# Page loads of the second cache set wait for half of the prompt's attention scores, not for all of them

## The chip, the cores and the metric

The kernel runs on one core of a Trainium2 chip. The metric is the device time of one execution in microseconds; lower is better. Three runs of the kernel before gave 1573.28, 1573.8 and 1576.76 us, so the median is 1573.8 us.

## The reference, cut to what matters

One layer of a hybrid decoder is computed for a prompt of 1040 tokens (16 meta tokens and 1024 of its own) and for 8 samples of 4 new tokens each. The part that matters here is the latent attention with 8 heads. For the prompt it is causal attention over its own tokens; for the samples it reads a paged cache of 4096 past tokens for each sample:

```python
def mla_sample(q_lat, q_rope, ckv_new, krope_new, cache_ckv, cache_krope, page_table):
    past_ckv = cache_ckv[page_table].reshape(Bd, -1, MLA_KV_LORA)      # 8 x 4096 x 256
    past_kr = cache_krope[page_table].reshape(Bd, -1, MLA_ROPE)        # 8 x 4096 x 32
    s_past = einsum('bthc,bsc->bhts', q_lat, past_ckv) + einsum('bthr,bsr->bhts', q_rope, past_kr)
    ...
    p = softmax(s * MLA_SCALE)
    return einsum('bhts,bsc->bthc', p[..., :P], past_ckv) + ...
```

Ahead of it stand the input projection and the gated linear attention, behind it the output projection, two normalisations and a gated feed-forward block with a short convolution.

## The kernel before, in words

Every engine runs one list of instructions, in order, and waits on semaphores (counters) that the others raise. Two stages matter.

**Prompt attention** (called d in the code). It has `N_ATT` = 66 steps: two for the last 16 tokens, and then, for each of 4 pairs of heads, 16 steps (8 blocks of 128 queries in the order 7, 0, 6, 1, 5, 2, 4, 3, for each of the two heads). In a step TensorE multiplies queries and keys (`scores`, L1268) and raises `score_done`; VectorE adds the mask and takes the maximum (L1389); ScalarE takes the exponentials (L1329) and raises `probs_done`; TensorE turns the probabilities (L1282); ScalarE and VectorE copy them out of PSUM (`ptb`, L1349 and L1402); and after both heads of a pair TensorE turns the reciprocals of the row sums (`rs`, L1291) and multiplies by the values (L1305). ScalarE then copies the reciprocals out of PSUM (`rb`, L1357), and VectorE multiplies them into the result (`catT`, L1435), which frees the bank for the next stage. TensorE issues scores two steps ahead of the step whose probabilities it turns. At the end of the stage there is no next step to run ahead with.

**Decode attention** (called e). The cache is read in `SETS` = 16 sets, z = 0 to 15; a set is 4 gathers of 512 KB (`load_latents`, L1534), one for each of 4 samples, issued by GpSimd (POOL), which also generates the descriptors. The rotary part comes in 4 groups of 4 gathers of 256 KB (`load_rotary`, L1541). A set lands in one of `SLOTS` = 3 slots `ring_c`, of 16 KB in each partition. The slots lie over memory of the stage before: slot 1 (sets 1, 4, ...) lies at `E0`, where `qT`, the prompt's queries, begins. `qT` has 8 heads of 4288 bytes, so slot 1 covers heads 0 to 3, all but the end of head 3. Slot 2 covers the rest of head 3 and most of the others.

For each set TensorE turns the pages (L1622), ScalarE and VectorE copy them out (`pastT`, L1727 and L1719), TensorE computes scores (L1643), turns the probabilities (L1655) and multiplies by the pages (L1669). Two steps on the samples' own new tokens come first. TensorE turns set 0 at once, and set 1 as the next step.

What GpSimd issues, in this order: the 4 gathers of set 0 (during the preparation of attention), `load_rotary(0)`, then a wait for `score_done` >= 33 and `load_rotary(1)`, then set 1, set 2, and so on, each behind `slot_free`. For set 1 that is a wait for all 66 scores, since the scores read `qT`. For set 2 the list has a wait of its own for `ss_done` >= 2, the first two scores of the decode stage. From set 3 on a slot is free when the values of the set in it are done.

Of the kernel before, what the change touches and what calls it, by code (L numbers as in the profile page):

```python
# [102 lines left out]
def build(nc, ins, outs):  # L103
    with ExitStack() as ctx:
# [8 lines left out]
        def sem(name):  # L113
            return ctx.enter_context(nc.semaphore(name))
# [1087 lines left out]
        score_done = sem("score_done")  # L1202
# [14 lines left out]
        N_ATT, N_JOBS = len(att_steps), len(att_jobs)  # L1217
# [290 lines left out]
        def step_of(z):  # L1508
            return z + 2
# [5 lines left out]
        def slot_free(eng, z):  # L1515
            if z == 0:

                eng.wait_ge(prep_done, index[("ckv", NT - 1)] + 1)
                eng.wait_ge(latent_stored, 96)
            if z == 1:  # L1520

                eng.wait_ge(score_done, N_ATT)
            if z >= SLOTS:

                eng.wait_ge(spv_done, step_of(z - SLOTS) + 1)
# [34 lines left out]
        def pool_e(pool):  # L1560
            pool.wait_ge(pages_ready, 2)
            slot_free(pool, 0)
            load_latents(0)
            out_of_psum(pool, prep[-1])
            load_rotary(0)
            pool.wait_ge(score_done, N_ATT // 2)
            load_rotary(1)
            for z in range(1, SETS):
                slot_free(pool, z)
                if z == 2:  # L1570
                    pool.wait_ge(ss_done, 2)
                if z < SLOTS:
                    load_latents(z)
                    continue
                load_latents(z, (0,))
                if 4 <= z < 12:
                    q = 1 + z // 4
                    if z % 4 == 0:
                        pool.wait_ge(rope_packed, R_SETS * (q - 1))
                    load_rotary(q, (z % 4,))  # L1580
                pool.wait_ge(ss_done, step_of(z - 2) + 1)
                load_latents(z, (1,))
                pool.wait_ge(past_turned, N_TURN * (z - 1) + 3)
                load_latents(z, (2,))
                pool.wait_ge(past_turned, N_TURN * (z - 1) + SPLIT_TURN)
                load_latents(z, (3,))
# [1482 lines left out]
```

## Time and profile before

| | |
|---|---|
| median of 3 runs | 1573.8 us |
| profiled execution, its own time | 1568.31 us |
| its span from first to last instruction | 1566.7 us |
| mean granted TensorE clock | 0.979 |
| TensorE busy | 95% of the span |
| prompt attention, from the first maximum to the last score | about 419 to 568 us |
| decode attention | about 577 to 743 us |

The durations below are from the profiled execution. It was 5.5 us (0.35%) shorter than the median of the runs, so a sum is made against 1568.31 and then carried over to 1573.8. In a row of the timeline the first number is the start in us from the start of the span, the second the duration in us; the brackets give how long the engine was idle before it and what ended the wait. "issue" and "remote" stand where the profile names no engine as the releaser.

### The profile page before, as it was taken

How to read it: one execution, taken by the hardware profiler on the slowest of the kernel's cores; microseconds unless marked ns; L12 is line 12 of the kernel's file. 1: busy time of each engine (PE TensorE's matmuls, PEld its weight loads, DVE VectorE, ACT ScalarE, POOL GpSimd, SP SyncE). 2: the span in 40 equal slices, each digit the busy share in tenths (PEclk: the TensorE clock that was granted, in tenths of full speed). 3: DMA queues.
4: the chain of work that ended last, by engine and by line, in shares of the span. 5: the costliest groups of instructions: out<-in, count | busy, mean ns of one | idle time of the engine just before them, and what ended most of it. 6: DMA issues, size and time to landing. Idle time of an engine off the chain costs nothing.

```text
span 1566.7 us, 29052 instructions
## 1 busy us (share of the span) xinstructions
PE 1486.0 (95%) x11025; PEld 1258.8 (80%) x11025; DVE 1002.7 (64%) x1733; ACT 655.6 (42%) x1232; POOL 346.1 (22%) x391
## 2 busy tenths in 40 slices
PE   5999999889899989999999999999999999999994
PEld 5989998656566666666788999999999998678883
DVE  6615302655455555556668888888888885456685
ACT  2255322543355543335222555555554443435330
POOL 2101000200000013441011144444444443110011
PEclk9999999889899999999999999999999999999997
DMA  7221101201100036776124255555555557978462
GB/s 259 82 69 59 55 28 42 72 4 54 42 1 28 1 107 216 238 245 219 68 94 110 82 188 185 173 178 167 184 180 177 168 175 258 359 237 307 151 200 94
DMA packets 121205, 217.63 MB, mean 139 GB/s; under 512 B 10922, under 2 KB 67880, under 8 KB 118264
## 3 DMA queue, kind: packets, MB, share of 16 engines
q1 hardware_dynamic: 97994, 120.89, 23.9%
q0 software_dynamic: 22976, 95.43, 17.4%
q8 instruction: 62, 1.02, 0.3%
q14 instruction: 29, 0.24, 0.0%
q10 hardware_dynamic: 144, 0.07, 0.0%
HBM read 165.66 MB, written 50.69 MB: 138 GB/s over the span
## 4 chain that ended last, share of the span: by engine, by line
PE 61%; DVE 6%; issue 3%; DMA 2%; ACT 1%; POOL 1%; SPq 0%; another core or an unknown queue 0%; ACTq 0%; DVEq 0%; POOLq 0%
PE ps L2280 9%; PE ps L2279 9%; PE ps L2278 9%; PE ps L1268 4%; PE ps L1622 3%; PE ps L2904 3%; PE ps L2906 3%; PE ps L2905 3%; PE ps L1643 3%; PE ps L1305 2%; PE ps L210 2%; PE ps L212 2%; PE ps L211 2%; PE ps L1282 2%; PE ps L1669 2%
## 5 line engine op out<-in xcount | busy, mean ns | idle before, releaser
L2278 PE MATMUL ps<-t_hi,op_hi 128*128 128x266 f32 (+1 forms) x672 | 192.2, 286 | 2.4 <-DVE gap_hi L2502 2.4
L2280 PE MATMUL ps<-t_hi,op_lo 128*128 128x266 f32 (+1 forms) x672 | 192.9, 287 | 0.0
L2279 PE MATMUL ps<-t_lo,op_hi 128*128 128x266 f32 (+1 forms) x672 | 192.7, 287 | 0.0
L210 PE MATMUL ps<-w_hi,hT_hi 128*128 128x256 f32 (+2 forms) x504 | 141.8, 281 | 3.4 <-DVE hT_lo L324 3.4
L2280 PE MATMUL ps<-h1T_hi,op_lo 128*128 128x266 f32 x504 | 144.1, 286 | 0.0
L2278 PE MATMUL ps<-h1T_hi,op_hi 128*128 128x266 f32 x504 | 143.5, 285 | 0.0
L2279 PE MATMUL ps<-h1T_lo,op_hi 128*128 128x266 f32 x504 | 143.4, 285 | 0.0
L212 PE MATMUL ps<-w_hi,hT_lo 128*128 128x256 f32 (+2 forms) x504 | 141.2, 280 | 0.0
L211 PE MATMUL ps<-w_lo,hT_hi 128*128 128x256 f32 (+2 forms) x504 | 141.1, 280 | 0.0
L2731 DVE TENSOR_TENSOR ring_lo<-d_raw,ring_hi 128x1024 fp32r<-128x1024 f32 x77 | 95.3, 1248 | 56.0 <-ACT ring_hi L2727 55.0
L2278 PEld LDWEIGHTS ps<-t_hi,op_hi 128*128 128x128 f32 x672 | 127.4, 190 | 2.6 <-DVE gap_hi L2502 2.6
L2727 ACT ACTIVATE ring_hi<-d_raw 128x1024 fp32r<-128x1024 f32 x77 | 81.7, 1061 | 112.2 <-DMA d_raw<-t_res 57.4
L2279 PEld LDWEIGHTS ps<-t_lo,op_hi 128*128 128x128 f32 x672 | 127.7, 190 | 0.0
L2280 PEld LDWEIGHTS ps<-t_hi,op_lo 128*128 128x128 f32 x672 | 127.4, 190 | 0.0
L2904 PE MATMUL ps<-ring_hi 128*128 128x512 f32 x308 | 121.6, 395 | 2.1 <-DVE ring_lo L2731 1.2
L2905 PE MATMUL ps<-ring_lo,ring_hi 128*128 128x512 f32 x308 | 120.2, 390 | 0.0
L2906 PE MATMUL ps<-ring_hi,ring_lo 128*128 128x512 f32 x308 | 119.9, 389 | 0.0
L2403 DVE TENSOR_TENSOR op_lo<-s_sum,op_hi 128x512 fp32r<-128x512 f32 x84 | 106.2, 1303 | 0.0
L1534 POOL DMA_INDIRECT ring_c<-in_cache_ckv,row_at x64 | 60.3, 942 | 188.7 <-PE ps L1268 69.9
L210 PEld LDWEIGHTS ps<-w_hi,hT_hi 128*128 128x128 f32 x504 | 96.8, 192 | 3.9 <-DVE hT_lo L324 3.8
L212 PEld LDWEIGHTS ps<-w_hi,hT_lo 128*128 128x128 f32 x504 | 97.3, 193 | 0.0
L211 PEld LDWEIGHTS ps<-w_lo,hT_hi 128*128 128x128 f32 x504 | 96.7, 192 | 0.0
(366 smaller groups left out, 3574.9 us busy)
## 6 DMA issues: line engine op xcount, KB each, us to landing
f_raw<-in_w_ffn_in SPq DMA_DIRECT2D x88, 256.0 KB, 3.3
g_res<-gap_lo SPq DMA_DIRECT2D x22, 528.0 KB, 3.6
g_mix<-in_w_down POOLq DMA_DIRECT2D x11, 1024.0 KB, 5.3
t_res<-g_mix POOLq DMA_DIRECT2D x11, 1024.0 KB, 4.2
g_mix<-g_res POOLq DMA_DIRECT2D x11, 1024.0 KB, 5.2
s_res<-g_mix POOLq DMA_DIRECT2D x11, 1024.0 KB, 4.2
d_raw<-in_w_down SPq DMA_DIRECT2D x22, 512.0 KB, 7.0
d_raw<-s_res SPq DMA_DIRECT2D x44, 256.0 KB, 3.6
```

The costliest lines, as they stand in the source:

```text
L210: nc.tensor.matmul(out, ah, bh, start=start, stop=False)
L211: nc.tensor.matmul(out, ah, bl, start=False, stop=False)
L212: return nc.tensor.matmul(out, al, bh, start=False, stop=stop)
L2278: nc.tensor.matmul(o, ah, bh, start=FIRST_IN[q] and k == 0, stop=False, skip_group_check=again)
L2279: nc.tensor.matmul(o, ah, bl, start=False, stop=False, skip_group_check=again)
L2280: last = nc.tensor.matmul(o, al, bh, start=False, stop=k == 3, skip_group_check=again)
L2403: nc.vector.tensor_tensor(op_lo[q][:, :, :], OP_OF[q], op_hi[q][:, :, :].bitcast(F32), sub).then_inc(op_split, 1)
L2727: nc.scalar.activation(ring_hi[m % RING][:, :], d_raw[raw_slot[m]][:, 0:1024], ACT.Copy).then_inc(d_high, 1)
L2731: nc.vector.tensor_tensor(ring_lo[m % RING][:, :], d_raw[raw_slot[m]][:, 0:1024], ring_hi[m % RING][:, :].bitcast(F32), sub).then_inc(d_sp ...
L2904: nc.tensor.matmul(b, ah, bh, start=j == 0 and not again, stop=False, skip_group_check=again)
L2905: nc.tensor.matmul(b, ah, bl, start=False, stop=False, skip_group_check=again)
L2906: last = nc.tensor.matmul(b, al, bh, start=False, stop=j == NJ - 1, skip_group_check=again)
```

## The change

Set 1 no longer waits for all 66 scores but for 2 + 33 = 35 of them. The two tail steps and the 32 steps of the first two head pairs come first, so once 34 scores are done nothing reads heads 0 to 3 of `qT` any more. Set 2, which had relied on set 1's wait standing ahead of it in the same list, gets the wait for all 66 scores itself.

```diff
             if z == 1:
 
+                eng.wait_ge(score_done, 2 + N_ATT // 2)
+            if z == 2:
+
                 eng.wait_ge(score_done, N_ATT)
             if z >= SLOTS:
```

No instruction is added, removed or put at another place in any engine's list. In GpSimd's list set 1 stands directly behind `load_rotary(1)` before and after; only the count that its first gather waits for differs, and the first gather of set 2 waits for two semaphores in place of one.

## Rows read from the trace of the kernel before

**Rows 1.** The page: busy time of the engines, then shares of the last chain
```profile
PE 1486.0 (95%) x11025; PEld 1258.8 (80%) x11025; DVE 1002.7 (64%) x1733; ACT 655.6 (42%) x1232; POOL 346.1 (22%) x391
...
PE 61%; DVE 6%; issue 3%; DMA 2%; ACT 1%; POOL 1%; SPq 0%; another core or an unknown queue 0%; ACTq 0%; DVEq 0%; POOLq 0%
```

**Rows 2.** Busy time by stretch: length, PE PEld DVE ACT POOL, clock, DMA, GB/s
```profile
540.00:555.00 15.00, 14.63 (x128) 10.53 (x125) 8.08 (x25) 8.25 (x26) 0.00 (x0) 1.00 0.01 2
...
640.00:680.00 40.00, 38.35 (x389) 23.96 (x388) 23.08 (x51) 14.97 (x34) 18.92 (x20) 1.00 0.75 241
```

**Rows 3.** Timeline of GpSimd: rotary group 1, set 1, set 2
```profile
493.51 0.95 POOL L1541 DMA_INDIRECT ring_r<-in_cache_krope,rope_at  x1 [79.46 <-PE ps L1268]
...
568.15 0.94 POOL L1534 DMA_INDIRECT ring_c<-in_cache_ckv,row_at  x1 [69.93 <-PE ps L1268]
...
578.72 0.94 POOL L1534 DMA_INDIRECT ring_c<-in_cache_ckv,row_at  x1 [5.88 <-PE ps L1643]
```

**Rows 4.** Busy time by microsecond, after set 1's gathers were issued
```profile
575.00:576.00 1.00, 1.00 (x14) 0.82 (x10) 0.00 (x0) 0.00 (x0) 0.00 (x0) 0.51 0.88 344
...
577.00:578.00 1.00, 0.92 (x40) 0.82 (x40) 0.61 (x3) 0.00 (x0) 0.00 (x0) 0.50 0.02 8
...
582.00:583.00 1.00, 1.00 (x11) 0.99 (x10) 0.53 (x1) 0.69 (x2) 0.69 (x2) 1.00 0.96 324
```

**Rows 5.** Timeline of TensorE, ScalarE and VectorE from prompt to decode attention
```profile
569.72 1.31 PE L1305 MATMUL ps<-ptb,v_h 128*64 128x128 f32 x20
570.96 0.66 PE L1282 MATMUL ps<-consts,probs 128*128 128x128 f32 x4
...
572.48 0.28 ACT L1357 ACTIVATE rb<-ps 128x128 f32<-128x128 f32 x1 [2.17 <-PE ps L1305]
572.86 0.29 DVE L1435 TENSOR_TENSOR catT<-ps,rb 128x128 f32<-128x128 f32 x1 [3.71 <-ACT rb L1357]
...
573.26 0.23 DVE L1417 COPY rs<-rinv 128x128 f32<-128x128 f32 x1
573.54 0.33 PE L1291 MATMUL ps<-consts,rs 128*128 128x128 f32 x1 [1.92 <-issue]
573.95 0.60 ACT L1349 ACTIVATE ptb<-ps 128x512 f32<-128x512 f32 x1 [1.20 <-remote]
574.60 1.62 PE L1305 MATMUL ps<-ptb,v_h 128*64 128x128 f32 x16 [0.74 <-ACT ptb L1349]
576.26 0.28 ACT L1357 ACTIVATE rb<-ps 128x128 f32<-128x128 f32 x1 [1.71 <-PE ps L1305]
...
577.08 0.44 PE L1643 MATMUL ps<-ckvT,qlat 128*32 128x32 f32 x16 [0.86 <-DVE catT L1435]
...
578.35 3.65 PE L1622 MATMUL ps<-consts,ring_c 128*128 128x128 f32 x16
...
589.25 1.97 PE L1622 MATMUL ps<-consts,ring_c 128*128 128x128 f32 x16
```

**Rows 6.** Timeline: the same value products within the attention, without a gather
```profile
534.57 1.31 PE L1305 MATMUL ps<-ptb,v_h 128*64 128x128 f32 x20
...
535.92 0.28 ACT L1357 ACTIVATE rb<-ps 128x128 f32<-128x128 f32 x1 [0.76 <-PE ps L1305]
...
503.66 1.09 PE L1305 MATMUL ps<-ptb,v_h 128*64 128x128 f32 x16
...
504.80 0.28 ACT L1357 ACTIVATE rb<-ps 128x128 f32<-128x128 f32 x1
```

**Rows 7.** Timeline of VectorE: first maxima of head pairs 2 and 3
```profile
499.27 1.23 DVE L1389 CUSTOM_DVE_ANT_0 ps<-ps,wide 128x1024 f32<-128x1024 f32 x1 [2.23 <-PE ps L1268]
...
501.77 1.23 DVE L1389 CUSTOM_DVE_ANT_0 ps<-ps,wide 128x1024 f32<-128x1024 f32 x1 [1.07 <-PE ps L1268]
...
534.12 1.23 DVE L1389 CUSTOM_DVE_ANT_0 ps<-ps,wide 128x1024 f32<-128x1024 f32 x1 [1.03 <-PE ps L1268]
...
537.83 1.23 DVE L1389 CUSTOM_DVE_ANT_0 ps<-ps,wide 128x1024 f32<-128x1024 f32 x1 [1.23 <-PE ps L1268]
```

## The prediction

> **What bounds the kernel now.** I read the page first. TensorE is busy for 95% of the span, and its work is by far the largest part of the chain that ended last [rows 1]. By stretches the same holds on both sides of the change: 14.63 of 15 us busy in the middle of the prompt attention with the DMA engines nearly still, 38.35 of 40 us in the decode attention at 241 GB/s [rows 2]. So a load can only matter where TensorE waits for it, or where it disturbs a hand-over on which TensorE waits.
>
> Next the timeline of GpSimd. Set 1's first gather was issued at 568.15, the end of a wait of 69.93 us for the last score [rows 3]. By the busy time of each microsecond its transfer still ran at 344 GB/s at 575 and was over at 577 (8 GB/s) [rows 4]. TensorE turns set 1 only at 589.25 [rows 5]. The set is ready 12 us before it is read. **As a load, the change saves nothing**: the 12 us of slack become about 80. Set 2 is issued at 578.72, released by the decode stage's own first scores [rows 3], and its new wait for score 66 was met 10 us before that. It costs nothing, even if the decode stage starts some us earlier.
>
> What is left is where the 2 MB of set 1 travel. Before, they travel between 568 and 577, exactly where the prompt attention runs out. There the timeline of the three engines shows two hand-overs that come late [rows 5]. The 20 value products start at 569.72 and last 1.31, so they end at 571.03; ScalarE's copy of the reciprocals, which waits for them, starts at 572.48. Within the attention, with no gather, the same pair is 534.57 + 1.31 = 535.88 and 535.92 [rows 6], so 0.04 us is usual and 1.41 us was lost. Then TensorE turns the last probabilities from 570.96 to 571.62, and ScalarE, free from 572.76, takes them only at 573.95.
>
> **The change, part by part.**
>
> 1. *The end of the prompt attention without a gather.* All by rows 5. The copy of the reciprocals would start at 571.03 + 0.04 = 571.07 and end at 571.35. VectorE's product followed its start by 0.38, and the end of the copy to `rs` (573.49) came 1.01 behind it: 572.08. ScalarE would take the turned probabilities at about 571.66, and end 0.60 later, at 572.26. In the trace the last 16 value products start 0.05 behind the end of that copy (573.95 + 0.60 = 574.55, then 574.60), so here at 572.31; `rs` at 572.08 would be turned by then or cost 0.1 more. That is 2.3 us less. The lower bound of this term is zero, if the late hand-overs have another cause; no row shows this place without a gather.
>
> 2. *The clock in it.* From 575 the granted clock is 0.51, then 0.50, that is 1.2 GHz, and it is back at 1.00 (2.4 GHz) in the row of 582 [rows 4]. Before it fell TensorE had idled 1.92 and 0.74 us [rows 5]. The last 16 value products took 1.66 us from their start to the copy that follows (574.60 to 576.26), against 1.14 (503.66 to 504.80) at the full clock [rows 6]: 0.5 us. The first 16 transposes of the decode stage took 3.65 us, those of set 1 at the full clock 1.97 [rows 5]: 1.7 us, of which I count 1.6, because copies out of PSUM then follow more closely. With term 1 the idle times shrink to about 0.5 and 0.8 us (the second is 576.26 + 0.28 to 577.08, of which nothing changes, and a little more). I take it that the clock holds then, so 2.1 us for this term; zero if it falls all the same.
>
> 3. *The same 2 MB within the attention.* The gather now goes out when 35 scores are done. The 35th is the first of head pair 2, whose maximum VectorE starts at 499.27 [rows 7]; GpSimd has issued the four of `load_rotary(1)` by then (from 493.51 on [rows 3]). So the first gather of set 1 is issued at about 499.4, and as the transfer before ended some 9 us after its first issue (568.15 to 577 [rows 3, 4]), this one ends at about 508. The trace has one gather just ahead of this place already, that of the rotary part, half as large. It too makes a hand-over late: VectorE starts the first maximum of pair 2 at 499.27, 2.50 us before the second at 501.77; in pair 3, without a gather, the distance is 534.12 to 537.83, so 3.71 [rows 7]. It came 1.21 us late, and the next one was on time, so it cost nothing: TensorE had two steps of scores to run ahead with. What is behind a late hand-over here is VectorE's maximum, ScalarE's exponentials and copies, and TensorE's turn of the probabilities two steps on. The price of 2 MB lies between nothing (as for the 1.21 us) and the whole of what they cost where there is no running ahead, 2.3 us. I take 0.4, near the row at the same place, because TensorE idles only 0.37 of 15 us [rows 2], and a hand-over that is 1.4 us or more late may exceed what it can cover.
>
> 4. *Rows that stay.* The instructions, their order, the bytes and the decode stage's own gathers are the same; 15 of 16 sets travel with the same neighbours.
>
> Sum: -2.3 - 2.1 + 0.4 = **-4.0 us**. Against the profiled execution that is 1568.31 to 1564.3; its distance to the median is taken as kept, so 1573.8 - 4.0 = **1569.8 us**, 0.25% less. About 0.2% (3.1 us) is what a measurement of this kernel can tell from no change, for the three runs alone spread over 3.5 us. The forecast is near that edge.
>
> The Trainium skill, "SBUF — State Buffer", section "SBUF: two separate sides", speaks against all of this. It says that engine ports and DMA ports to that memory are disjoint and cannot contend. By that rule a gather delays no compute, the late hand-overs of rows 5 and 7 must have another cause, and terms 1 to 3 are all nothing. The trace does not agree with it taken widely: it shows late starts in both places. But it may be right about the memory, if what is late is the signal.
>
> **The rivals.**
>
> *The clock falls all the same.* For it: about 1.3 us of idle time remain within 3 us. Against it: smaller idle times within the attention leave 1.00 [rows 2]. Then only terms 1 and 3 count, with or without the 0.5: -1.9 to -2.4, so 1571.4 to 1571.9 us.
>
> *Nothing happens.* The set was hidden before and is hidden after, and the late hand-overs belong to the drain of a stage (or to the taking of the profile) and not to the gather; this is also the case by the skill's rule above. For it: two of the three late ones stand at the drain. Against it: the third stands in the steady part, and there, too, a gather is under way. 1573.8 us, give or take 1.
>
> *Slower.* The gather's late hand-overs fall into the attention and are not covered. The place is the four or five steps from 499 to 508, where TensorE is the bound. If each of the four gathers delays one hand-over by up to 2.3 us with nothing to run ahead with, that is 9.2 us; less the gain at the end (4.4) it is +4.8, so 1578.6 us. The point from which it decides is a loss of 4.4 us there for any slowdown, and of 7.5 us for one that can be measured. Against it: the 1.21 us of rows 7 were covered in full.
>
> *In between.* The gain at the end is real, and the loss in the attention eats half of it or all: 1571.5 to 1573.8 us.
>
> **How the numbers follow.** Forecast as summed: 0.38. Clock falls all the same: 0.19. Nothing: 0.22. In between: 0.11. Slower: 0.10. Of the forecast and the clock case 0.40 lie beyond 0.2% on the fast side. Of the other cases a tenth of the whole may come out beyond it on the slow side, and a little more by scatter between measurements; I say faster 0.40, same 0.47, slower 0.13. The range runs from 1568 (term 3 at nothing, and a little of the decode start) to 1576.5 (half of the slower case, and scatter of the median), and leaves out the rest of the slower case and the far ends. The forecast's own range is 1568 to 1571.
>
> **What the new profile would show.** GpSimd issues set 1 from about 499.4 on. In the last steps of the prompt attention the copy `rb` follows the value products by 0.04 us, ScalarE's last `ptb` follows the turn at once, and the decode scores start about 2.8 us earlier, measured from the last score. The clock stays at 1.00 there, and the first 16 transposes take about 2 us. Between 499 and 508 some maximum or copy starts over 1 us late, but the distance from the first maximum of pair 2 to that of pair 3 grows by no more than 1 us. The forecast is wrong if the drain has the same late hand-overs without a gather in it, if the clock falls anyway, or if pair 2 grows by 3 us or more.

## The result, and the profile after

The changed kernel took **1576.88 us** (median of 20 runs, 1572.2 to 1582.97), the kernel before 1573.26 us (20 runs, 1569.24 to 1576.76). The ratio is **1.0031, 95% interval 1.0021 to 1.0042**; the two medians alone give 1.0023, the two means 1.0032. That is 0.2 to 0.3% slower where 0.25% faster was forecast, and 0.4 us outside the stated range. Two later comparisons of the same two kernels gave 0.9998 and 0.9997, and the kernel before against its own copy gave 1.0018 and 0.9997. So the change is a small loss to nothing, not the gain of 4 us. It does move time about inside the kernel, and that can be read in the traces, though each trace is one execution only.

The profiled execution took 1580.67 us. The page gives for it, as [rows 1] for before, the busy time of the engines and the shares of the last chain:

```profile
PE 1493.1 (95%) x11025; PEld 1263.9 (80%) x11025; DVE 1000.7 (63%) x1733; ACT 655.6 (42%) x1232; POOL 346.5 (22%) x391
...
PE 61%; DVE 6%; issue 2%; DMA 2%; ACT 1%; POOL 1%; SPq 0%; another core or an unknown queue 0%; ACTq 0%; DVEq 0%; POOLq 0%
```

Totals tell nothing here: the same work, a span 12.4 us longer, of which 5.4 had gathered before the prompt attention began (its first maximum starts at 425.36, against 419.93). What the change does is read from distances within one trace: from the first maximum at L1389 on VectorE, which is that of the first head pair, to the first decode score; from the last maximum to it; and from it to the end of the last product with the pages.

| one profiled execution | first maximum to decode | last maximum to decode | decode to last product |
|---|---|---|---|
| before | 157.15 | 9.16 | 165.98 |
| changed | 160.14 | 6.44 | 167.34 |

**The end of the attention.** The timeline of TensorE and ScalarE in the changed kernel, where [rows 5] stood before:

```profile
580.87 1.31 PE L1305 MATMUL ps<-ptb,v_h 128*64 128x128 f32 x20
582.11 0.66 PE L1282 MATMUL ps<-consts,probs 128*128 128x128 f32 x4
582.23 0.28 ACT L1357 ACTIVATE rb<-ps 128x128 f32<-128x128 f32 x1 [0.76 <-PE ps L1305]
...
582.81 0.60 ACT L1349 ACTIVATE ptb<-ps 128x512 f32<-128x512 f32 x1 [0.30 <-PE ps L1282]
...
583.29 0.33 PE L1291 MATMUL ps<-consts,rs 128*128 128x128 f32 x1 [0.52 <-DVE rs L1417]
583.55 1.09 PE L1305 MATMUL ps<-ptb,v_h 128*64 128x128 f32 x16
584.69 0.28 ACT L1357 ACTIVATE rb<-ps 128x128 f32<-128x128 f32 x1 [1.28 <-PE ps L1305]
...
585.50 0.33 PE L1646 MATMUL ps<-ckvT,qlat 128*32 128x32 f32 x16 [0.86 <-DVE catT L1435]
...
586.42 1.97 PE L1625 MATMUL ps<-consts,ring_c 128*128 128x128 f32 x16
```

The products end at 582.18 and the copy `rb` starts 0.05 behind them, where it was 1.45 behind. The last 16 products take 1.14 to the copy behind them, where it was 1.66, and the transposes of set 0 take 1.97, where it was 3.65. The clock did not fall. The end of the attention is 9.16 - 6.44 = 2.72 us shorter; 2.8 had been worked out.

**The attention.** GpSimd's timeline has set 1 directly behind the rotary gathers, and set 2 again behind the decode stage's first scores ([rows 3]):

```profile
503.97 0.95 POOL L1537 DMA_INDIRECT ring_c<-in_cache_ckv,row_at  x1 [0.31 <-issue]
...
587.29 0.94 POOL L1537 DMA_INDIRECT ring_c<-in_cache_ckv,row_at  x1 [78.63 <-PE ps L1646]
```

And the timeline of the three engines at that time:

```profile
503.51 1.23 DVE L1389 CUSTOM_DVE_ANT_0 ps<-ps,wide 128x1024 f32<-128x1024 f32 x1 [1.03 <-ACT probs L1329]
...
503.95 1.31 PE L1305 MATMUL ps<-ptb,v_h 128*64 128x128 f32 x20
...
505.20 1.98 PE L1268 MATMUL ps<-kT,qT 96*128 96x512 f32 x4
...
507.02 0.60 PE L1282 MATMUL ps<-consts,probs 128*128 128x128 f32 x4
...
510.37 0.28 ACT L1357 ACTIVATE rb<-ps 128x128 f32<-128x128 f32 x1 [5.15 <-remote]
...
510.75 0.29 DVE L1435 TENSOR_TENSOR catT<-ps,rb 128x128 f32<-128x128 f32 x1 [5.94 <-ACT rb L1357]
510.95 1.22 DVE L1389 CUSTOM_DVE_ANT_0 ps<-ps,wide 128x1024 f32<-128x1024 f32 x1
...
511.79 0.49 PE L1268 MATMUL ps<-kT,qT 96*128 96x128 f32 x2 [4.17 <-ACT probs L1329]
```

Three pieces of TensorE's work end at 505.26, 507.18 and 507.62 by their rows (the ends of matmuls are modelled). What waits for the first, the copy `rb`, starts at 510.37, with ScalarE idle for 5.15 us and VectorE for 5.94. TensorE then idles 4.17 us itself. The running ahead by two steps was used up. In what follows, "a late signal" stands for this: an engine takes up a result of TensorE long after the row of that work ends. In these rows a signal that came late can't be told from a result that was finished late. By the busy time of each microsecond, TensorE had nothing to do at 509 and the clock fell behind it:

```profile
509.00:510.00 1.00, 0.00 (x0) 0.00 (x0) 0.00 (x0) 0.00 (x0) 0.00 (x0) 1.00 1.11 352
...
512.00:513.00 1.00, 1.00 (x7) 1.00 (x7) 0.75 (x6) 0.96 (x2) 0.00 (x0) 0.63 0.36 148
513.00:514.00 1.00, 1.00 (x6) 0.70 (x4) 0.08 (x1) 0.96 (x3) 0.00 (x0) 0.50 0.03 12
```

Ahead of head pair 2, and from the maximum at 516.54 up to the last one, the distances between neighbouring maxima equal those of before to 0.01 us. So the loss lies in this one place: 160.14 - 157.15 + 2.72 = 5.7 us. Of these, 3.8 are there at the maximum at 510.95, and 2.0 more come up to that at 516.54, while the clock was down. The late start of 1.21 us at the rotary gathers ([rows 7]) is missing in this trace, though the same gathers run: the first maximum of pair 2 follows the last of pair 1 by 503.51 - 501.25 = 2.26 us, against 499.27 - 495.80 = 3.47 before. Where a signal is late is not the same in every execution.

**The decode stage's start.** It gives back part of the gain at the end:

```profile
590.72 0.63 PE L1672 MATMUL ps<-zt,spt 32*32 32x256 f32 x8
...
592.96 0.27 ACT L1730 ACTIVATE spt<-ps 32x128 f32<-32x128 f32 x1 [2.09 <-remote]
593.12 0.42 DVE L1850 COPY oacc<-ps 128x256 f32<-128x256 f32 x1 [0.81 <-remote]
...
593.70 0.66 PE L1672 MATMUL ps<-zt,spt 32*32 32x256 f32 x8 [2.35 <-DVE oacc L1850]
594.28 3.54 PE L1646 MATMUL ps<-pastT,qlat 128*32 128x512 f32 x16
```

```profile
595.00:596.00 1.00, 1.00 (x10) 0.20 (x5) 0.42 (x2) 0.00 (x0) 0.00 (x0) 0.50 1.03 410
```

While set 2 travels (410 GB/s), TensorE's results are taken late again: it idles 2.35 us, and the scores of set 0 then take 3.54 us at a granted clock of 0.50, that is 1.2 GHz; the trace of before has them in 1.92 us at 586.40. The decode part is 1.36 us longer than before although its first transposes were 1.7 us quicker.

### The profile page after: what moved, and what is told of

Same layout as the page of the kernel before. It is cut to its first block, busy times and chain, and to the rows that moved or that the text cites. A ratio compares the mean times of both kernels' runs of the same rounds, so it can differ in the third digit from the quotient of the medians.

```text
span 1579.1 us, 29053 instructions
## 1 busy us (share of the span) xinstructions
PE 1493.1 (95%) x11025; PEld 1263.9 (80%) x11025; DVE 1000.7 (63%) x1733; ACT 655.6 (42%) x1232; POOL 346.5 (22%) x391
## 2 busy tenths in 40 slices
DMA packets 121205, 217.63 MB, mean 138 GB/s; under 512 B 10922, under 2 KB 67880, under 8 KB 118264
## 4 chain that ended last, share of the span: by engine, by line
PE 61%; DVE 6%; issue 2%; DMA 2%; ACT 1%; POOL 1%; SPq 0%; another core or an unknown queue 0%; ACTq 0%; DVEq 0%; POOLq 0%
PE ps L2283 9%; PE ps L2282 9%; PE ps L2281 9%; PE ps L1268 4%; PE ps L1625 3%; PE ps L1646 3%; PE ps L2907 3%; PE ps L2908 3%; PE ps L2909 3%; PE ps L210 2%; PE ps L212 2%; PE ps L211 2%; PE ps L1305 2%; PE ps L1672 2%; PE ps L1282 2%
```

## The experiments

They stand in four groups; each group was timed against the kernel before, on one chip. The kernel before had two levels: 1563.57 us (group 1) and 1563.53 (group 3), 1573.00 (group 2) and 1573.94 (group 4), each group on another chip. In all traces of groups 1 and 3 no signal of TensorE around set 1 is late, in groups 2 and 4 there are late ones. As each chip was met once, chip and moment can't be told apart; "on such chips" below means in such a group. This split turned out to be the main finding, so the groups are told in order. "Distance" is that from the first maximum to the first decode score.

### Group 1: place, amount and issuer

**apart50**: set 1 behind 50 scores.

```diff
             if z == 1:
-                eng.wait_ge(score_done, 2 + N_ATT // 2)
+                eng.wait_ge(score_done, 50)
```

> The changed kernel with the 4 gathers of set 1 waiting for 50 scores (two and three pairs of steps done) instead of 35, so that about 35 us lie between the rotary gathers and them. Measure: the distance from the first masked maximum of the prompt attention to the first decode score, 157.15 us in the kernel before and 160.14 in the changed one, and the latest signal of TensorE in the gather. Theory backlog (the stall of 5 us comes from 2 MB issued right behind the 1 MB of the rotary part): no signal over 1.5 us late, distance about 154.5, total 1570 to 1571. Theory bytes (any 2 MB in one go stall TensorE's signals by some 5 us in the attention): distance about 160, total 1576 to 1577 as in the changed kernel.

**spread**: one gather at a time.

```diff
+                if z == 1:
+                    for b in range(4):
+                        pool.wait_ge(score_done, 38 + 6 * b)
+                        load_latents(z, (b,))
+                    continue
```

> The changed kernel with the 4 gathers of set 1 one by one, behind 38, 44, 50 and 56 scores. Theory backlog and theory bytes both: each gather of 512 KB makes a signal at most about 1 us late, which TensorE's lead of two steps covers; distance from first maximum to first decode score about 154.3 (157.15 less the 2.8 of the undisturbed end), total 1570 us. If it is still 158 or more, the stall hangs on a single gather meeting a single moment and not on how much is in flight.

**sp_direct**: plain copies from SyncE. A semaphore of its own, `sp_loaded`, replaces the first round of slot 1's (the edits of TensorE's waits are left out here).

```diff
+            sp.wait_ge(score_done, 2 + N_ATT // 2)
+            for b in range(4):
+                sp.dma_start(ring_c[1][:, b, :, :].rearrange("p j c -> p (j c)"),
+                             ins["cache_ckv"].rearrange("n (p j) c -> (n p) (j c)", j=4)[P * b:P * b + P, :]).then_inc(sp_loaded, 16)
```

> The changed kernel, but the 2 MB of set 1 are loaded by 4 plain copies of 512 KB from SyncE, behind the same 35 scores, from pages 0 to 15 in order: set 1 holds other pages than the table asks for, so its part of the decode attention is computed on other data. Theory descriptors (GpSimd's generation of descriptors, or its gathers as such, hold TensorE's signals): no late signal but the 1.2 us of the rotary gathers, distance about 154.5, total 1570. Theory traffic (2 MB at about 350 GB/s hold them, whoever issues them): late by 3 to 5 us again, distance about 159 to 160, total 1576.

**swap**: set 1 first, the rotary gathers later.

```diff
-            pool.wait_ge(score_done, N_ATT // 2)
+            slot_free(pool, 1)
+            load_latents(1)
+            pool.wait_ge(score_done, 50)
             load_rotary(1)
-            for z in range(1, SETS):
+            for z in range(2, SETS):
```

> The changed kernel with set 1's gathers behind 35 scores, and the rotary gathers of group 1 moved behind them, to 50 scores. Theory backlog: with nothing ahead of them, the 2 MB make signals at most 1.5 to 2.3 us late; distance 154.5 to 156, total 1570 to 1572. Theory bytes: late by 5 us, distance about 160, total about 1576.

| group 1 | median of 12 | ratio, interval | distance | last maximum to decode | decode to last product |
|---|---|---|---|---|---|
| apart50 | 1565.41 | 1.0010 (0.9997 to 1.0024) | 153.98 | 6.44 | 162.44 |
| spread | 1563.64 | 0.9998 (0.9982 to 1.0013) | 154.01 | 6.44 | 162.47 |
| sp_direct | 1563.84 | 1.0002 (0.9990 to 1.0013) | 153.98 | 6.44 | 162.37 |
| swap | 1563.63 | 0.9999 (0.9988 to 1.0011) | 153.98 | 6.44 | 162.47 |

Nothing told the theories apart. The stall was absent in all four, but so was the late signal of the rotary gathers, which none but swap had touched. All were 3.2 us shorter in the attention than the trace of before, yet none was faster than the kernel before on that chip. That only fits if the kernel before has no late signals there either.

### Group 2: the same two kernels again

Copies of the two kernels, and two edits: **thrice** and **sp_drain**, which is sp_direct with `score_done >= N_ATT` in its wait. The edit of thrice, without that of TensorE's counts:

```diff
+                if z == 1:
+                    load_latents(z)
+                    for b in range(2):
+                        pool.wait_ge(set_loaded[1], 32 * (b + 1))
+                        pool.wait_ge(late_loaded[1], 32 + 32 * (b + 1))
+                        load_latents(z)
+                    continue
```

before_again: 

> The kernel before, once more, with a profile. The four kernels run so far all had 153.98 us from the first maximum to the first decode score, the rotary gathers' late signal of 1.2 us was missing in them, and their totals were those of the kernel before on the same chip. Theory chip (late signals of TensorE depend on the chip or the moment, not on the kernel): the kernel before shows none here either, neither at 498 nor at the end of the attention, distance about 154, and the end takes 6.44 us from the last maximum to the first decode score instead of 9.16. Theory kernel (they come with the gathers, wherever it runs): 1.2 us late at the rotary gathers, 1.4 and 2.3 at the end, distance 157.

after_again: 

> The changed kernel, once more. Theory chip: distance 153.98, ratio to the kernel before 1.000 within 0.15%. Theory kernel: a stall of some 5 us behind score 35 again, distance about 160, ratio about 1.003.

thrice: 

> The changed kernel with set 1 gathered three times over into the same slot, each time behind the landing of the last, so that 6 MB travel in the attention in place of 2. Theory chip: nothing late, distance 153.98, ratio 1.000. Theory kernel (a share of the gathers stalls TensorE's signals): three times as many chances, some stall of over 2 us, distance 158 or more.

sp_drain: 

> Set 1 loaded at the end of the attention as in the kernel before (behind all 66 scores), but by 4 plain copies from SyncE and from pages 0 to 15 in order, so its part of the decode attention is computed on other data. If the two late signals at the end come from GpSimd's gathers: from the last maximum to the first decode score 6.44 us. If they come from 2 MB of traffic: 9.2 us. Theory chip: 6.44 us here and in the kernel before.

| group 2 | median of 11 or 12 | ratio, interval | distance | last maximum to decode | decode to last product |
|---|---|---|---|---|---|
| before_again | 1575.53 | 1.0018 (1.0006 to 1.0029) | 157.54 | 9.55 | 168.42 |
| after_again | 1572.95 | 0.9998 (0.9987 to 1.0010) | 155.53 | 6.44 | 167.39 |
| thrice | 1574.42 | 1.0014 (1.0000 to 1.0028) | 157.33 | 6.44 | 168.46 |
| sp_drain | 1571.40 | 0.9987 (0.9972 to 1.0002) | 154.05 | 6.44 | 167.78 |

Here the late signals are back. The timeline of before_again repeats [rows 5]:

```profile
570.06 1.31 PE L1305 MATMUL ps<-ptb,v_h 128*64 128x128 f32 x20
...
572.85 0.28 ACT L1357 ACTIVATE rb<-ps 128x128 f32<-128x128 f32 x1 [2.20 <-PE ps L1305]
...
574.32 0.60 ACT L1349 ACTIVATE ptb<-ps 128x512 f32<-128x512 f32 x1 [1.20 <-remote]
...
577.81 0.44 PE L1643 MATMUL ps<-ckvT,qlat 128*32 128x32 f32 x16 [0.86 <-DVE catT L1435]
```

`rb` starts 1.48 us behind the products (570.06 + 1.31). In sp_drain, in the same group and at the same place, plain copies carry the same number of bytes while those products are handed over; its timeline and the busy time of its stretch:

```profile
570.71 1.31 PE L1305 MATMUL ps<-ptb,v_h 128*64 128x128 f32 x20
...
572.07 0.28 ACT L1357 ACTIVATE rb<-ps 128x128 f32<-128x128 f32 x1 [0.76 <-PE ps L1305]
...
575.35 0.33 PE L1656 MATMUL ps<-ckvT,qlat 128*32 128x32 f32 x16 [0.86 <-DVE catT L1435]
```

```profile
571.00:573.00 2.00, 1.61 (x24) 1.20 (x20) 0.52 (x3) 0.93 (x3) 0.00 (x0) 1.00 0.94 373
```

The copy is 0.05 behind, at 373 GB/s. So on this chip, in one trace of each, **2 MB of traffic alone make nothing late; as many bytes by GpSimd's gathers do**. after_again kept to neither of its theories: the distance is 1.1 us over the 154.4 that is undisturbed on such chips (worked out in group 4), neither 153.98 nor 160. thrice lost 157.33 - 154.4 = 2.9 us in the attention for 6 MB, in two places. Its expectation of 158 or more was missed by a little, and the stall of 5 us wasn't in it in one piece.

### Group 3: again, with the kernel before

spread_2: 

> Set 1's four gathers one by one behind 38, 44, 50 and 56 scores, once more. The first four kernels met no late signal at all and the second four met some in every kernel with gathers, at another level of the kernel before (1563.6 and 1573.0 us). Theory gathers: where late signals occur (kernel before near 1573), a gather of 512 KB alone makes them at most 1 us late, so the distance from first maximum to first decode score is 154 to 155, the end 6.44, and the ratio to the kernel before 0.997 to 0.999. Where they don't occur (near 1564): 153.98 and 1.000, as before. Rival backlog-free stall (a single gather can stall for 5 us): distance 158.

swap_2: 

> Set 1 behind 35 scores with the rotary gathers moved to 50, once more. Where late signals occur: if the backlog behind the rotary gathers makes the large stall, distance 154 to 155.5 and ratio 0.998; if 2 MB by themselves do, 156 to 160 and ratio 1.000 to 1.003. Where they don't occur: 153.98 and 1.000.

sp_direct_2: 

> Set 1 by plain copies from SyncE behind 35 scores, from pages 0 to 15 in order (its part of the decode attention is computed on other data), once more. Where late signals occur: theory descriptors says only the 1.2 us at the rotary gathers, which costs nothing, so 153.98 and a ratio of about 0.998; theory traffic says 155.5 to 160. Where they don't occur: 153.98 and 1.000.

before_3: 

> The kernel before, a third profile and a second timing against itself. The ratio tells how far two loads of one program differ: the first such pair gave 1.0018. I expect 0.999 to 1.002. The end of the attention takes 9.2 to 9.6 us if its total is near 1573, and 6.44 if it is near 1564.

| group 3 | median of 12 | ratio, interval | distance | last maximum to decode | decode to last product |
|---|---|---|---|---|---|
| spread_2 | 1563.41 | 0.9992 (0.9978 to 1.0007) | 153.99 | 6.43 | 162.45 |
| swap_2 | 1564.55 | 1.0002 (0.9989 to 1.0015) | 153.99 | 6.43 | 162.45 |
| sp_direct_2 | 1563.74 | 0.9994 (0.9979 to 1.0009) | 153.99 | 6.43 | 162.38 |
| before_3 | 1563.24 | 0.9997 (0.9983 to 1.0011) | 154.05 | 6.50 | 162.43 |

before_3 is the row that group 1 lacked: the unchanged kernel, with set 1's gathers at the end of the attention. Its timeline and its busy time by microsecond:

```profile
572.20 1.31 PE L1305 MATMUL ps<-ptb,v_h 128*64 128x128 f32 x20
...
573.56 0.28 ACT L1357 ACTIVATE rb<-ps 128x128 f32<-128x128 f32 x1 [0.76 <-PE ps L1305]
...
574.13 0.60 ACT L1349 ACTIVATE ptb<-ps 128x512 f32<-128x512 f32 x1 [0.30 <-PE ps L1282]
...
574.94 1.09 PE L1305 MATMUL ps<-ptb,v_h 128*64 128x128 f32 x16
...
576.90 0.33 PE L1643 MATMUL ps<-ckvT,qlat 128*32 128x32 f32 x16 [0.86 <-DVE catT L1435]
```

```profile
573.00:574.00 1.00, 1.00 (x14) 0.69 (x10) 0.07 (x1) 0.28 (x1) 0.87 (x1) 1.00 0.97 344
...
575.00:576.00 1.00, 1.00 (x17) 0.79 (x16) 0.00 (x0) 0.00 (x0) 0.30 (x1) 1.00 1.01 356
```

The gathers run at 344 and 356 GB/s beside the hand-overs, and `rb` is 0.05 behind. On this chip the change has nothing to win: 9.16 is already 6.50. The three variants met no late signal either, so what they were to tell apart stayed open; swap did not run where signals are late.

### Group 4: the variants where signals are late

after_3: 

> The changed kernel, a third profile and timing. If the kernel before is near 1563.5 in this comparison (no late signals): distance from the first maximum to the first decode score 153.99, end 6.44 us, ratio 1.000 within 0.15%. If it is near 1573 (late signals): distance 155 to 160, end 6.44, ratio 1.000 to 1.003.

spread_3: 

> Set 1's gathers one by one behind 38, 44, 50 and 56 scores. Near 1563.5: 153.99 and 1.000. Near 1573: each gather of 512 KB is late by at most 1 us, distance 154 to 155, ratio 0.997 to 0.999.

apart50_2: 

> Set 1's four gathers together behind 50 scores, 35 us behind the rotary ones. Near 1563.5: 153.99 and 1.000. Near 1573: if 2 MB of gathers in one go make the loss, distance 155.5 to 158; if it took the rotary gathers right ahead of them, 154 to 154.5.

sp_direct_3: 

> Set 1 by plain copies from SyncE behind 35 scores, from pages 0 to 15 in order (its part of the decode attention is computed on other data). Near 1563.5: 153.99 and 1.000. Near 1573: 154 if GpSimd's gathers make the signals late (as at the end of the attention, where plain copies left 6.44 us), 155.5 or more if any traffic does.

| group 4 | median of 12 | ratio, interval | distance | last maximum to decode | decode to last product |
|---|---|---|---|---|---|
| after_3 | 1574.09 | 0.9997 (0.9983 to 1.0011) | 155.44 | 6.44 | 167.66 |
| spread_3 | 1571.70 | 0.9980 (0.9967 to 0.9993) | 154.41 | 6.44 | 168.18 |
| apart50_2 | 1571.76 | 0.9983 (0.9969 to 0.9997) | 155.34 | 6.44 | 167.66 |
| sp_direct_3 | 1570.63 | 0.9977 (0.9961 to 0.9993) | 154.44 | 6.44 | 165.94 |

The undisturbed distance here is 154.4, not 153.98. The 0.4 us lie between the first two maxima, and every kernel of groups 2 and 4 but sp_drain (154.05) has them in full. No transfer runs there, and the clock differs. The busy time right behind the first maximum, in after_3 (it starts at 420.64) and then in apart50 (at 418.89):

```profile
420.00:421.00 1.00, 1.00 (x4) 0.60 (x3) 0.36 (x1) 0.00 (x0) 0.00 (x0) 0.50 0.00 0
...
419.00:420.00 1.00, 0.75 (x8) 0.51 (x7) 1.00 (x1) 0.60 (x1) 0.00 (x0) 1.00 0.00 0
```

In sp_drain the clock is back at 0.89 in the microsecond of its first maximum. I therefore put the 0.4 us down to the clock and not to set 1. So set 1 in the attention costs 1.0 us in after_3 and nothing in spread_3 and sp_direct_3. In after_3 the timeline shows the usual form of the loss:

```profile
503.01 0.49 PE L1268 MATMUL ps<-kT,qT 96*128 96x128 f32 x2
...
503.34 1.08 PE L1282 MATMUL ps<-consts,probs 128*128 128x128 f32 x8
...
505.96 0.30 DVE L1389 CUSTOM_DVE_ANT_0 ps<-ps,wide 128x128 f32<-128x128 f32 x1 [1.34 <-remote]
...
506.02 0.60 ACT L1349 ACTIVATE ptb<-ps 128x512 f32<-128x512 f32 x1 [0.44 <-remote]
```

Scores that ended at 503.50 are taken up by VectorE at 505.96, 2.46 us behind their end. VectorE had other work for the first 1.1 us of that and then idled for 1.34. The step has only 128 keys, so I take it that there is little other work to cover the wait. In sp_direct_3 the copies run in the same steps without a loss; its busy time:

```profile
506.00:508.00 2.00, 1.97 (x20) 1.49 (x21) 1.96 (x7) 1.59 (x2) 0.00 (x0) 1.00 0.98 385
508.00:510.00 2.00, 2.00 (x25) 1.82 (x20) 0.71 (x4) 1.76 (x7) 0.00 (x0) 1.00 1.01 406
```

In spread_3 GpSimd's timeline has the gathers 12 to 16 us apart; two of the four:

```profile
510.39 0.94 POOL L1537 DMA_INDIRECT ring_c<-in_cache_ckv,row_at  x1 [7.75 <-PE ps L1268]
524.74 0.94 POOL L1537 DMA_INDIRECT ring_c<-in_cache_ckv,row_at  x1 [13.41 <-PE ps L1268]
```

In apart50_2 the four together, 34 us behind the rotary ones, still cost 0.9 us. The backlog behind the rotary gathers is therefore not needed for a loss of this size; whether it is for the 5.7 us was not seen:

```profile
534.78 1.31 PE L1305 MATMUL ps<-ptb,v_h 128*64 128x128 f32 x20
...
538.03 0.28 ACT L1357 ACTIVATE rb<-ps 128x128 f32<-128x128 f32 x1 [2.65 <-remote]
...
539.46 0.49 PE L1268 MATMUL ps<-kT,qT 96*128 96x128 f32 x2 [1.01 <-ACT probs L1329]
```

Of the versions that compute the reference, spread has the shortest distance where signals are late. By time it can't be told from apart50_2 (0.9980 and 0.9983, with intervals that overlap), whose distance is 0.9 us longer; without late signals it gave 0.9998 and 0.9992. Its gain is no larger than what the kernel before showed against itself (1.0018), so it rests on the distance, of one trace, as much as on the ratio.

## Why the prediction was wrong

**Right: the load was hidden, and what counts is where it travels.** No trace shows a wait for set 1 in either kernel.

**Right: term 1 and the half microsecond of term 2, the end of the attention.** Forecast 2.3 + 0.5 = 2.8, measured 2.72, and 6.44 us in every kernel whose set 1 is not gathered there. That the gathers are the cause where signals are late is shown by sp_drain and before_again in one group; before_3, with 6.50 us, shows that gathers alone are not enough.

**Wrong in its size, and the step that failed: term 3, "I take 0.4, near the row at the same place".** It measured 5.7 us in the profile of the first comparison, 1.1 and 1.0 in the two others (155.53 and 155.44 less 154.4). The upper bound was the weak point: 2.3 us was what the 2 MB had cost at the end of the attention, where only two signals were there to be late. A signal can be 5.1 us late (505.26 to 510.37), so "the whole of what they cost where there is no running ahead" bounded nothing. The 1.21 us of [rows 7], covered in full, led me to weigh the lead of two steps too highly. Of the signs that the prediction named for being wrong, one came in full (and the clock fell, if one stretch later): from the first maximum of pair 2 to that of pair 3 it is 41.76 us in the changed kernel against 34.86, so 6.9 more (1.2 of them because that first maximum was late before and is not here), where 3 was the mark. In the two other profiles it is 1.1 more.

**Half wrong: term 2, the 1.6 us of the first transposes.** They came (3.65 to 1.97), but no gain of the decode stage as a whole is shown: 167.34, 167.39 and 167.66 us lie between the two of the kernel before where signals are late, 165.98 and 168.42. Set 2's gathers meet the same kind of hand-overs, and in the changed kernel the clock fell one stretch later. From the first decode score to the turning of set 1 it is 9.97 us in before_3, 2.2 more in before, 4.3 more in before_again and 3.3 more in the three traces of the changed kernel. Term 4 took the cost of the decode stage's own gathers as unchanged; it differs from one trace of the same kernel to the next by more than the 1.6 us that were at stake. I had not priced the next gather in line.

**The sum where signals are late.** The changed kernel's own profile: +2.99 + 1.36 = +4.4 us, with a ratio of 1.0031, which is 4.9 us. after_3 against the trace of before: -1.71 in the distance, +1.68 in the decode part, together 0.0, with a ratio of 0.9997, but these traces come from two chips. The one pair from one chip, after_again against before_again, gives -2.01 - 1.03 = -3.0 us, while the median of after_again is equal to that of the kernel before (1572.95 and 1573.00) and 2.6 us below that of its copy. So one trace gives such a sum to some 3 us only, and that the first one agrees with its ratio is in part luck: that execution took 1580.67 us, 3.8 above the median. The slower rival (0.10) named this place and this mechanism, and the first comparison came out its way; the two later ones, 0.9998 and 0.9997, came out as "nothing" or the upper end of "in between".

**The rival "nothing happens"** fits the quiet group of before_3: there the end of the attention is short already. The changed kernel itself was not run on a quiet chip, only variants of it, all at the level of the kernel before. The reason is one that the rival did not have: the late signals are absent there before and after. The rule of the Trainium skill ("SBUF — State Buffer", section "SBUF: two separate sides") comes out better than I had it. Engines ran undisturbed beside 344 to 406 GB/s of traffic in before_3, sp_drain and sp_direct_3. What is late are hand-overs from TensorE, on some chips, during gathers. My reading of the rule, by which terms 1 to 3 would all be nothing, fails where they are late: the end of the attention got 2.7 us shorter.

**Open.** Why chips, or moments, differ (1563.5 against 1573 to 1574 us for one program). Whether it is the generated descriptors, the order of the addresses (the plain copies took pages that lay in order) or the queue that sets a gather apart from a plain copy. The number and the bytes of the packets do not: the profiles of before and sp_drain both have 121205 packets and 217.63 MB, and set 1's 576 packets (2.1 MB) only stand in the hardware queue in place of the software one. And how often the stall of 5 us comes; it was in one of three profiles of the changed kernel. The first comparison's 1.0031 was not met again, and since two copies of one program differed by 0.18%, with an interval (1.0006 to 1.0029) that leaves out 1, part of it may belong to that one load of the program.

## What to carry to other kernels

A transfer that nobody waits for still has a price where engines hand work to each other, so try to spread gathers over steps with work to run ahead with rather than issue 2 MB at once (one trace, no loss against 1.0 us); and when one is moved away, look at what the next one behind it will meet. Bound a disturbance by the longest wait that it could cause, not by the sum seen where only two hand-overs were exposed. Before a forecast of 0.2%, time the unchanged kernel against its own copy, and on more than one chip.

## What the runs showed of the hardware

- One program ran at two levels, 1563.5 and 1573 to 1574 us, each on two chips, with each chip met once. In single profiles the attention is 3.1 us longer at the upper level and the decode part 3.6 us or more (154.05 and 162.43 in before_3; 157.15 and 165.98 in before), both with late hand-overs from TensorE while gathers are under way.
- TensorE's own work kept its schedule during a late hand-over: in the changed kernel the value products ran from 503.95 to 505.26 by their row and the next scores began at 505.20, while ScalarE waited from 505.22 to 510.37 for the former. Only when two steps of lead were used up did TensorE stop, for 4.17 us, and the granted clock went from 1.00 to 0.50 behind it.
- Plain copies of 512 KB from SyncE moved 373 GB/s in sp_drain beside the same hand-over with a delay of 0.05 us, and 385 and 406 GB/s in sp_direct_3 without a loss in the distance.
